# Two token sets taken apart at every norm of a transformer block on one core

## The reference

```python
def modulate(h, shift, scale):
    return h * (1 + scale[:, None, :]) + shift[:, None, :]
...
        x = x + 0.5 * mx[2][:, None] * swiglu(modulate(rms_norm(x), mx[0], mx[1]), ffn1_w_gu[layer], ffn1_w_down[layer])
        ctx = ctx + 0.5 * mc[2][:, None] * swiglu(modulate(rms_norm(ctx), mc[0], mc[1]), ffn1_w_gu[layer], ffn1_w_down[layer])

        hx = modulate(rms_norm(x), mx[3], mx[4])
        hc = modulate(rms_norm(ctx), mc[3], mc[4])
...
        x = x + mx[5][:, None] * merge_mixers(ax, upx, ufx, pool_w[layer], pool_scale[layer], fft_w[layer], w_out[layer])
        x = x + 0.5 * mx[8][:, None] * swiglu(modulate(rms_norm(x), mx[6], mx[7]), ffn2_w_gu[layer], ffn2_w_down[layer])
...
    return rms_norm(x) * final_gain
```

## Time and profile before

| | us |
|---|---|
| median of 3 runs (2538.87 to 2546.56) | 2544.44 |
| the profiled execution, its own time | 2544.74 |
| its span, first to last instruction | 2543.0 |
| PE busy / weight loads busy | 2335.4 / 1824.4 |
| DVE / ACT / POOL busy | 1144.9 / 745.8 / 292.6 |
| mean granted TensorE clock | 0.956 |

### The profile page before, as it was taken

One profiled execution on the slowest core, in us unless ns is written; L12 is line 12 of the kernel. 1 busy time (PEld: TensorE's weight loads), 2 busy tenths in 40 slices (PEclk: granted clock), 3 DMA queues, 4 the chain that ended last, 5 costly groups with the idle time before them and its releaser, 6 DMA issues.

```text
span 2543.0 us, 32043 instructions
## 1 busy us (share of the span) xinstructions
PE 2335.4 (92%) x13009; PEld 1824.4 (72%) x13009; DVE 1144.9 (45%) x1608; ACT 745.8 (29%) x994; POOL 292.6 (12%) x304
## 2 busy tenths in 40 slices
PE   6998988999959999988898999998999999878998
PEld 5877974545438888857456788886787787747998
DVE  4678544343343333352533533334533334555555
ACT  5445321111132222132441321222322222344333
POOL 2120050000020000121333000004000003102001
PEclk9999988999979999999988999999999999888999
DMA  8785776999643233224682224324224324204564
GB/s 257 239 271 172 245 285 256 419 421 420 282 122 100 80 111 89 85 83 166 223 274 66 66 73 118 99 75 114 67 73 119 100 68 123 83 1 114 160 183 124
DMA packets 379565, 408.63 MB, mean 161 GB/s; under 512 B 11866, under 2 KB 344015, under 8 KB 364335
## 3 DMA queue, kind: packets, MB, share of 16 engines
q1 hardware_dynamic: 356912, 327.01, 39.2%
q0 software_dynamic: 22064, 79.09, 9.3%
q10 hardware_dynamic: 462, 0.70, 0.1%
HBM read 405.71 MB, written 1.05 MB: 160 GB/s over the span
## 4 chain that ended last, share of the span: by engine, by line
PE 84%; DVE 9%; ACT 3%; DMA 2%; issue 1%; POOL 0%; SPq 0%; DVEq 0%; POOLq 0%; ACTq 0%
PE B L1558 21%; PE B L1560 21%; PE B L1559 21%; PE B L1868 5%; PE B L1888 3%; PE B L1663 2%; PE B L1837 2%; PE B L1825 2%; DVE R L648 1%; DVE hL L643 1%; PE B L1651 1%; DVE LO L637 1%; DMA HF<-in_ada_w 1%; DVE hH L642 1%; DVE R L1017 1%
## 5 line engine op out<-in xcount | busy, mean ns | idle before, releaser
L1558 PE MATMUL B<-hH,HI 128*128 128x512 f32 (+1 forms) x1808 | 645.5, 357 | 71.8 <-DVE hL L643 59.2
L1560 PE MATMUL B<-hH,LO 128*128 128x512 f32 (+1 forms) x1808 | 636.3, 352 | 2.1 <-issue 2.1
L1559 PE MATMUL B<-hL,HI 128*128 128x512 f32 (+1 forms) x1808 | 636.8, 352 | 0.0
L1170 ACT ACTIVATE HI<-RAW 128x2048 fp32r<-128x2048 f32 (+3 forms) x219 | 371.7, 1697 | 781.8 <-PE B L1560 758.2
L637 DVE TENSOR_TENSOR LO<-RAW,HI 128x2048 fp32r<-128x2048 f32 (+3 forms) x219 | 452.9, 2068 | 234.3 <-ACT HI L1170 232.0
L1558 PEld LDWEIGHTS B<-hH,HI 128*128 128x128 f32 x1808 | 348.0, 192 | 139.8 <-issue 67.4
L1560 PEld LDWEIGHTS B<-hH,LO 128*128 128x128 f32 x1808 | 348.9, 193 | 46.8 <-issue 2.5
L1559 PEld LDWEIGHTS B<-hL,HI 128*128 128x128 f32 x1808 | 349.4, 193 | 42.9 <-issue 0.5
L1045 DVE TENSOR_TENSOR T<-B,T 128x512 f32<-128x512 f32 (+1 forms) x88 | 55.0, 625 | 482.4 <-PE B L1560 482.4
L1558 PE MATMUL B<-aH,HI 128*128 128x512 f32 (+1 forms) x704 | 258.6, 367 | 2.5 <-DVE LO L637 2.4
L1560 PE MATMUL B<-aH,LO 128*128 128x512 f32 (+1 forms) x704 | 257.8, 366 | 0.0
(11 more groups left out here) (316 smaller groups left out, 2858.9 us busy)
## 6 DMA issues: line engine op xcount, KB each, us to landing
RAW<-in_ffn_w_gu SPq DMA_DIRECT2D x176, 512.0 KB, 5.0
W<-in_w SPq DMA_DIRECT2D x78, 1024.0 KB, 12.3
HF<-in_ada_w POOLq DMA_DIRECT2D x108, 512.0 KB, 7.2
W2T<-in_w SPq DMA_DIRECT2D x39, 1024.0 KB, 12.5
RAW<-in_w_in SPq DMA_DIRECT2D x62, 512.0 KB, 4.9
RAW<-in_ffn_w_down SPq DMA_DIRECT2D x56, 384.0 KB, 3.2
ADW<-in_ada_w POOLq DMA_DIRECT2D x36, 512.0 KB, 7.6
RAW<-in_ffn_w_down SPq DMA_DIRECT2D x56, 320.0 KB, 3.7
```

Source lines behind the costliest of these rows:

```text
L1170: A.activation(HI[s % HI_SLOTS][:, :words], RAW[s][:, :words], ACT.Copy).then_inc(hi_done[s], 1)
L1558: mm(o, wh, xh, start=first, stop=False, **more)
L1559: mm(o, wh, xl, start=False, stop=False, **more)
L1560: return mm(o, wl, xh, start=False, stop=last, **more)
```

## The change

1. **Last tiles of a stage per token set.** In the second half of an FFN on both sets, down tiles 6 and 7 are made for x first (banks 6 and 7), then for ctx (banks 4 and 5). In layer 0 the mixers' output tiles 4 to 7 likewise. Both chunks stay in their HI slots until ctx is done.
2. **First two chunks of the next stage per token set**, x before ctx (in the first FFN ctx before x).
3. **The norm per token set.** POOL squares tiles 0 to 5 (EVEN = 6), ACT tiles 6 and 7 of each set; three 256-column mean matmuls per set, x's placed inside the first ctx tile after its fifth k-step, ctx's ahead of the second tile of the next stage. DVE's product takes the modulation's scale along, ACT adds the shift while making hH, DVE's second instruction makes hL with the shift; POOL's multiplications and the copy go. The next stage's first chunk is split in halves, LO between the products.
4. **Experts to FFN.** Chunks 0 and 1 of the first FFN are issued after y of the second-last pair; their RAW slots (0, 1) are W2T's, the router's scratch goes to slots 2 and 3. ctx's mean is made ahead of pair 0, its norm in the last two pairs; ACT and DVE split chunk 0 in the last pair. x's squares are taken by pairs of tiles and summed in bank 4 behind the first ctx tile.
5. **Loops unrolled.** All `Fori` loops (SP, POOL, DVE, ACT, PE) are written out. The unused chunk behind the last FFN is gone.

```diff
@@ PE: a half tile, a half mean
+            def mean_of_half(v, b, acc, sq):
+                claim(b, "std_ready")
+                o = B[b][:, v * S:(v + 1) * S]
+                if acc:
+                    got("acc_ready")
+                mm(o, mat(MEAN_D), ACC[:, v * S:(v + 1) * S], start=True, stop=False)
+                for i in range(KT - EVEN):
+                    got("sq_ready")
+                    ins = mm(o, mat(MEAN_D), sq[:, i * S:(i + 1) * S], start=False, stop=(i == KT - EVEN - 1))
+                ins.then_inc(E["stats_done"], 1)
+
+            def half_tile(b, v, wh, wl, xh, xl, fresh=None, beside=None):
+                cols, last = slice(v * S, (v + 1) * S), len(wh) - 1
+                for k in range(last + 1):
+                    if fresh:
+                        fresh(k)
+                    ins = exact(B[b][:, cols], wh[k], wl[k], xh[:, k, cols], xl[:, k, cols], k == 0, k == last)
+                    if beside and k == 4:
+                        beside()
+                return ins
@@ PE: the end of an FFN, after its last loop
+                for i, (s, b, wh, wl) in enumerate(ends):
+                    claim(b, "x_ready")
+                    half_tile(b, 0, wh, wl, aH, aL).then_inc(E["part_done"], 1)
+                for i, (s, b, wh, wl) in enumerate(ends):
+                    stat = (lambda: mean_of_half(0, 3, True, T[5])) if i == 0 else None
+                    claim(b - 2, "x_ready")
+                    used(half_tile(b - 2, 1, wh, wl, aH, aL, None, stat), s)
@@ PE: the stages in order
+            claim(0, "std_ready")
+            got("acc_ready")
+            mm(B[0][:, S:], mat(MEAN_D), ACC[:, S:], start=True, stop=True).then_inc(E["stats_done"], 1)
...
+            into_ffn((1, 0), mean_of_pairs, 1)
+            ffn(2 * S, True)
+            mixers(0)
+            into_ffn((0, 1), lambda: mean_of_half(1, 4, True, T[2]))
+            ffn(2 * S, True)
+            into_ffn((0, 1), lambda: mean_of_half(1, 3, False, T[2]))
+            ffn(2 * S, True)
+            mixers(1)
+            into_ffn((0,), None)
+            ffn(S, False)
@@ DVE: the norm and what surrounds it
+            def low(l, shift, k, v, h):
+                got("hf_ready")
+                cols = slice(v * S, (v + 1) * S)
+                V.scalar_tensor_tensor(hL[:, k, cols], h, MOD[:, l, shift * KT + k, v:v + 1],
+                                       hH[:, k, cols].bitcast(F32), ALU.add, ALU.subtract).then_inc(E["h_ready"], 1)
+
+            def norm(l, shift, scale, v, first, beside):
+                cols = slice(v * S, (v + 1) * S)
+                rstd(R[0][:, cols])
+                for p in first:
+                    p()
+                for k in range(KT + 2):
+                    if k < KT:
+                        V.scalar_tensor_tensor(HF[:, k, cols], XC[:, k, cols], MOD[:, l, scale * KT + k, v:v + 1],
+                                               R[0][:, cols], ALU.mult, ALU.mult).then_inc(E["xn_ready"], 1)
+                    if k >= 2:
+                        low(l, shift, k - 2, v, HF[:, k - 2, cols])
+                    for p in beside.get(k, ()):
+                        p()
...
+            def into(l, shift, scale, before, then, late, both):
+                s = t.take()
+                def part(i):
+                    prep_part(s, CHUNK // 2 * i, CHUNK // 2 * (i + 1))
+                for p in before:
+                    p()
+                norm(l, shift, scale, 0, then, {0: [lambda: part(0)], 3: [lambda: part(1)], 5: late})
+                prep()
+                if both:
+                    norm(l, shift, scale, 1, [], {})
...
+                prep(FFN_CHUNKS[-1])
+                for m in range(EVEN, KT):
+                    x_part(m)
+                into(l2, shift, scale, [], [lambda: ctx_part(EVEN)], [lambda: ctx_part(EVEN + 1)], True)
@@ ACT: the norm and what surrounds it
+            def high(l, shift, k, v, h):
+                got("xn_ready")
+                A.activation(hH[:, k, v * S:(v + 1) * S], h, ACT.Identity, bias=MOD[:, l, shift * KT + k, v:v + 1])\
+                    .then_inc(E["hf_ready"], 1)
...
+            def into(l, shift, bank, both):
+                last_squares(0, T[5])
+                root(B[bank][:, 0:S], R[0][:, 0:S])
+                s = take()
+                for i in range(2):
+                    prep_part(s, CHUNK // 2 * i, CHUNK // 2 * (i + 1))
+                norm(l, shift, 0)
+                if both:
+                    t.n["x_ready"] += both - (KT - EVEN)
+                    last_squares(1, T[2])
+                prep()
+                if both:
+                    root(B[bank][:, S:], R[0][:, S:])
+                    norm(l, shift, 1)
@@ ACT and DVE: the expert pairs
+            root(B[0][:, S:], R[1][:, S:])
...
+                if i == PAIRS - 1:
+                    prep()
...
+                    if i == PAIRS - 1:
+                        for k in range(4 * half, 4 * half + 4):
+                            low(0, 0, k, 1, HFC[:, k, :])
...
+                if i == PAIRS - 2:
+                    for k in range(KT):
+                        V.scalar_tensor_tensor(HFC[:, k, :], XC[:, k, S:], MOD[:, 0, KT + k, 1:2], R[1][:, S:],
+                                               ALU.mult, ALU.mult).then_inc(E["xn_ready"], 1)
@@ SP
-                with t.loop(2, ring_counts(t.pos, len(FFN_CHUNKS), "fill")) as half:
+                for half in range(2):
                     for j in range(FT_HALF):
+                        if l == 0 and gu == "ffn1_w_gu_2" and half == 0 and j == 2:
+                            sp.wait_ge(E["acc_done"], 1)
...
-            sp.wait_ge(E["acc_done"], 1)
+            sp.wait_ge(E["y_done"], 2 * (PAIRS - 1))
...
-            columns(w_in, 0)
```

More of the change, by code:

```diff
@@ L76, in __init__ @@
     def __init__(self, eng):
-        self.eng, self.n, self.turn, self.per = eng, Counter(START), None, {}
+        self.eng, self.n = eng, Counter(START)
         self.pos = self.used = 0
     def at(self, key, back=0):
[L81 to L84, removed]
+        return self.n[key] - back
     def next(self, key, by=1):
@@ L88, in next @@
         return self.at(key)
[L90 to L100, removed]
     def take(self):
@@ L544, in ada_weights @@
                 if i1 - i0 > 1:
-                    with t.loop(i1 - i0 - 1, {f"ada_used{place}": 1 for place in range(4)}) as i:
-                        two_steps(i + (i0 + 1), False, None)
+                    for i in range(i0 + 1, i1):
+                        two_steps(i, False, None)
             def inputs_used():
@@ L596, in _ @@
             t.n["x_ready"] += KT // 2
[L597 to L606, removed]
-                if l + 1 < LAYERS:
-                    norm(n)
-            squares(KT - 1, S, by_tile)
+            after_ffn(2)
+            pool.wait_ge(E["pf_ready"], 4)
+            ada_weights(1, 0, ADA_STEPS // 2, False, None)
+            even_squares_in_turn()
+            after_ffn(2)
+            after_ffn(2)
+            even_squares(1)
+            after_ffn(1)
         @block.vector
@@ L1384, in ffn @@
+            for j in range(4):
+                got("x_ready")
+                A.activation(T[2 + j][:].rearrange("p (a n) -> p a n", a=2), XC[:, 2 * j:2 * j + 2, 0:S], ACT.Square).then_inc(E["sq_ready"], 1)
+            prep()
+            root(B[4][:, :S], R[0][:, :S])
+            norm(0, 0, 0)
             def ffn(n):
-                counts = {**ring_counts(t.used, len(FFN_CHUNKS), "used", "fill"), "gated": FT_HALF, "gate_done": FT_HALF}
-                with t.loop(2, counts):
+                for half in range(2):
@@ L1551, in chunk, with rest @@
                 return s
+            def rest(s):
+                pe.wait_ge(lo_done[s], t.next(f"split{s}"))
             def used(ins, s):
@@ L1891, in _, with gate_up @@
             scatter(PAIRS - 1).then_inc(E["acc_done"], 1)
-            def ffn(n):
-                counts = {**ring_counts(t.pos, len(FFN_CHUNKS), "fill", "split"), "silu_ready": FT_HALF, "gated": FT_HALF,
-                          "hid_ready": FT_HALF, "x_ready": KT}
-                normed = t.n["h_ready"]
-                t.n["h_ready"] += KT
-                with turns(2, counts, ["silu_ready", "gated", "x_ready"]):
+            def gate_up(s):
+                wh, wl = slot(s, k=2 * KT)
+                return [[[w[:, which * KT + k, :] for k in range(KT)] for w in (wh, wl)] for which in range(2)]
@@ L1900, in ffn @@
+            def ffn(n, stagger):
+                for h in range(2):
                     for j in range(FT_HALF):
+                        if h == 0 and j < 2:
+                            continue
                         s = chunk()
@@ L2053, in mixers @@
                 pe.wait_ge(E["mix_ready"], t.n["mix_ready"])
-                for j in range(4):
+                for j in range(4 if n == S else 2):
                     s = chunk()
```

410 lines of the change are left out of this document (259 added, 151 removed).

## The result

The changed kernel takes **2472.75 us** (median of 4 runs, 2471.59 to 2473.87) against 2541.65 (4 runs, 2533.15 to 2546.56): a ratio of 0.9732, 95% interval 0.9704 to 0.9761. The forecast was 2468, its range 2449 to 2492. The profiled execution took 2473.87, span 2472.0, so 70.9 less than the one before, where my sum had 76.4.

A forecast was written before the change was run, and what follows sets the result against it. The prediction took TensorE's work plus its holes, chiefly waits for hL at stage boundaries, to bound the kernel. Boundary gains, unrolling and a 2.0 us loss summed to 76.4 us: 2544.7 to 2468 us, 8-in-10 range 2449 to 2492.

The forecast's parts named there:

- FFN to mixers and FFN to FFN: Boundaries FFN to mixers of layer 0 and FFN 2 to FFN 1 of layer 1: gains of 8.2 and 8.0 us.
- x halves of tiles 6 and 7 end at 3.9 and 7.9: FFN to mixers, layer 0: when the x halves of the last two down tiles end, in us after tile 5.
- The new wait for hL: FFN to mixers, layer 0: the next stage's first x tile finishes 4.1 us late, waiting for the norm's last hL.
- Mixers to FFN 2, layer 0: Boundary from layer 0's mixers to its FFN 2: 66.3 us falls to 51.5, counted as a gain of 14 us.
- The expert end: Experts to FFN 1 of layer 0: gain 35.4 us, with early chunks 0 and 1 costing nothing if landed by 695.
- FFN 1 to mixers, layer 1: Boundary in layer 1, up to chunk 2: PE starts chunk 2 at 42.4 instead of 48.6, a gain of 6.2 us.
- Unrolling: Writing out the loops removes issue waits of 2.08 and 4.30 us at layer 1's second turns: gain 5.6 us.
- The price of a cut: Cutting tiles costs 0.012 us per matmul pair with hH, 0.006 in down and out tiles; 6.4 us in all.
- rival (2): Half tiles load weights twice and may cost more per matmul: slower, 2563 us, chance 0.02; milder form 2509, chance 0.02.
- (1): In-order queues: VectorE regularly late, so the four halved boundaries give half, 18 us less: 2486 us; chance 0.14.
- (3): Straight-line code waits for instructions, 3 us each, ten times, 30 us: 2498 us; chance 0.05.
- (4): More gain: PE never falls to its lower clock at boundaries, norm at 0.74 us per tile: 2445 us; chance 0.12.

The follow-up runs named there:

- e1: Changed kernel, but TensorE waits for LO of tile 7's chunk only after issuing tile 6's x half: 2457.77 us, ratio 0.9677.
- e3: Changed kernel with the first FFN's chunks 0 and 1 held until the last scatter is done: 2487.90 us, ratio 0.9795.
- e5: e1 with chunk 2's HI and LO in layer 1's mixers made earlier, and TensorE starting chunk 2 with x: 2452.99 us, ratio 0.9654.
- e4: Changed kernel with gate and up tiles of all 20 middle chunks of each wide FFN also cut in halves: 2514.65 us, ratio 0.9900.
- e7: e1 plus the changes of e5 and e6, and ctx's mean at the start of the experts in bank 7: 2445.36 us, ratio 0.9622.
- e8: e7 with about twice the filler matmuls, and 9 or 7 more between the first products behind x's norm: 2443.18 us, ratio 0.9626.
- e6: e1 with fp32 matmuls of a constant into an unread bank where TensorE would stand idle: 2450.41 us, ratio 0.9637.
- e2: Kernel before the change with all its engine loops written out and nothing else: 2523.67 us, ratio 0.9939.
- e10: Kernel before the change with only the FFNs' loops written out on SyncE, VectorE, ScalarE and TensorE: 2527.49 us, ratio 0.9955.

## Why the prediction was right, and where it was not

**The whole.** 71 of 76 us came, by the mechanism forecast: the waits for hL shrank from 59 to 14 us, and the wait of 18.6 us behind the scatter went. It was nearer than its steps deserved, for two errors of about 12 and 6 us pointed in opposite directions. That is luck.

**FFN to mixers and FFN to FFN.** The step that failed is "x halves of tiles 6 and 7 end at 3.9 and 7.9". It took for granted that tile 6 starts at once. I had followed the HI slots held by chunks 6 and 7 forward to the norm's chunk and not back to chunk 7 itself, whose split needs tile 5's slot and whose wait TensorE takes first. The halves ended at 10.4 and 14.2 us after tile 5's residual (1065.95 and 1069.81 against 1055.58). Of the loss some 3.7 us are the wait and 2.8 the clock behind it; e1 gives 15 us back over three boundaries and lands on the sum's own figures, 7.8 and 8.7 for 8.2 and 8.0. The norm's unit costs were sound: products and lows came at 0.79 us per tile for my 0.8.

**The new wait for hL** was 4.1 us late by my sum. The waits that the trace names are 1.6 (1.31 and 0.27 in e1), but the first x tile is 4.6 us late (7.5 for 2.9), so the term was about right. Its cause was not all as I had it: the last hL was there at 22.8 in e1, for my 23.9, and the clock took part. At mixers to FFN 2 of layer 0 I had 2 us, and the tile took 6.8 (1348.16 to 1354.95), 3.9 late.

**Mixers to FFN 2, layer 0**: 14.5 for 14. There PE takes the wait for an end chunk only when it comes to that chunk's first half tile, so nothing stood in front of the half tiles. The expert end: 35.9 for 35.4, with the chunk at 693.19 inside the forecast's 695; e3 shows that the early first chunks carried 15 of it.

**FFN 1 to mixers, layer 1**: 5.4 for 6.2 looks right and is two errors: the late tile 6 cost some 3.8 (e1: 39.1 us to chunk 2 in place of 42.9), and the sum's 42.4 was 3.3 too long. The wait before chunk 2, forecast as "some 7 us", was 4.3, and e5 takes it away.

**Unrolling**: 5.6 was read off the two labels. The trace gives 9.6 at the same two turns, and the runs 12 for the FFN loops and up to 6 for GpSimd's. I had counted the hole and not the clock that falls behind it (0.50 for 5 us), the thing I had pointed to at the norms. The Trainium skill's rule (Runtime: NRT & Kernel Launch, Instruction fetch mechanics) could put a cost on every turn; layer 0's two cost nothing, 127.4 us with and without the loop, and no run places the rest.

**Start of the experts**: 1.1 for 2.0; the root's wait was 1.28.

**The price of a cut.** 0.0134 to 0.0145 us per pair for my 0.012, 1 to 3 us in all. The half tiles are 52, not the 56 that rival (2) counts; its 1356 half matmuls are right.

**The rivals.** (1), in-order queues late by half, gave 2486; something like it happened at two boundaries, but from one misplaced wait, not from a full VectorE, as e1 and e5 show. (2) is excluded by e4. (3), instruction waits in straight code, would have claimed the three waits called issue; e1 shows that they were not that. (4), no fall of the clock, did not come; e7 and e8 are what it would have taken.

## What to carry to other kernels

When a tile is cut so that a chain starts earlier, follow every wait that stands in program order ahead of the first piece: a loop that collects operands for several tiles takes all their waits before it issues anything. Price a hole on TensorE with the slow stretch that can follow it: behind three equal holes of 3.7 us it was 2.8, 1.8 and 0.2 us here. And a wait that seems to be a full queue may be only its order; one experiment that moves the late item forward tells.

## What was not expected of the hardware

- A profile's issue label on a wait of 3.68 us that ended 0.1 us behind another engine's instruction, three times, and went when that wait was moved.
- The granted clock falls in stretches where no single hole is over 1.7 us (1195 to 1215 in the changed kernel: 1.63, 1.65 and shorter ones, 5.6 of 20 us idle), and with six fp32 matmuls on a constant (twelve records) it stayed at 1.00.
- Three equal holes of 3.68 us were followed by a clock of 0.58, 0.70 and 1.00.
- One fp32 matmul of 256 columns is two records of 0.215 us in the trace (22 for 11 in e6); a 256-column matmul of the split operands is one, every 0.119 us.
- The kernel before differs by 14 us from run to run with its clock's mean, 0.953 to 0.961. The five executions of e2 spread over 4.5 us, the six of e10 over 9.3, so it is open whether the loops do it.
